# Two-layer hybrid attention and mixture-of-experts kernel: softmax inverse sums spread on VectorE and turned by one transpose; last token tile of the mixing stage done by halves

## What is computed

```python
s = jnp.concatenate([s_loc.reshape(bsz, rows, GRID_W, H, n_loc), s_ctx], axis=-1)
p = jax.nn.softmax(s, axis=-1).astype(v.dtype)
out = (jnp.einsum('brqhkw,brkwhd->brqhd', p_loc, vb)
       + jnp.einsum('brqhk,bkhd->brqhd', p_ctx, v_ctx))
```

```python
x = x + g1 * merge_branches(...)
h2 = modulate(rmsnorm(x, norm2_g[l]), sh2, sc2).reshape(bsz * L, d)
s = jax.nn.sigmoid((h @ router_w).astype(jnp.float32))   # then top-1 group, top-2 experts
```

## Time and profile before

| | us |
|---|---|
| median of 3 runs | 3292.83 (3286.64 to 3298.44) |
| the profiled execution, its own time | 3285.09 |
| its span, first to last instruction | 3283.3 |
| TensorE busy | 3161.9 (96%), 16228 matmul passes |
| VectorE busy | 1649.9 (50%) |
| ScalarE busy | 891.3 (27%) |
| GpSimd busy | 858.3 (26%) |
| mean granted TensorE clock | 0.984 of full |
| attention, first layer | about 380 to 550 |
| attention, second layer | about 2129 to 2282 |
| last tile of mixing, first layer | 1202 to 1222 |
| last tile of mixing, second layer | 2759 to 2779 |

### The profile page before, as it was taken

The page is one execution under the profiler, slowest core; times in us unless marked ns, Lnnn a source line. Parts: engine busy times, 40 slices in busy tenths (PEclk is TensorE's granted clock), DMA queues, the critical chain, the costliest instruction groups (busy, mean ns, idle before and its releaser), DMA issues. The chain is left out here.

```text
span 3283.3 us, 47029 instructions
## 1 busy us (share of the span) xinstructions
PE 3161.9 (96%) x16228; PEld 2440.5 (74%) x16229; DVE 1649.9 (50%) x2422; ACT 891.3 (27%) x1675; POOL 858.3 (26%) x536
## 2 busy tenths in 40 slices
PE   7999999999999999999999999999999989999998
PEld 5887688777777887667666888688778778666665
DVE  4562366666632576433544565166222246887640
ACT  4321265111111332222222332156112132222222
POOL 0140000111011125444444023000111112676664
PEclk9999999999999999999999999999999998999999
DMA  6122243344424246656787522152111134798853
GB/s 263 56 90 106 85 132 97 130 132 135 132 65 153 97 167 227 231 175 210 257 281 249 186 77 103 63 147 85 52 43 51 47 139 181 279 341 285 286 177 83
DMA packets 157387, 500.45 MB, mean 152 GB/s; under 512 B 30498, under 2 KB 81314, under 8 KB 133924
## 3 DMA queue, kind: packets, MB, share of 16 engines
q1 hardware_dynamic: 110880, 394.83, 32.6%
q0 software_dynamic: 17568, 59.82, 8.0%
q10 hardware_dynamic: 28804, 43.98, 4.3%
HBM read 422.51 MB, written 76.39 MB: 152 GB/s over the span
## 5 line engine op out<-in xcount | busy, mean ns | idle before, releaser
L218 PE MATMUL wide<-part,part 128*128 128x512 f32 (+2 forms) x2416 | 974.5, 403 | 28.2 <-DVE part L2632 13.8
L220 PE MATMUL wide<-part,part 128*128 128x512 f32 (+2 forms) x2416 | 929.3, 385 | 0.0
L219 PE MATMUL wide<-part,part 128*128 128x512 f32 (+2 forms) x2384 | 915.2, 384 | 0.0
L218 PEld LDWEIGHTS wide<-part,part 128*128 128x128 f32 x2416 | 458.2, 190 | 139.0 <-issue 47.0
L219 PEld LDWEIGHTS wide<-part,part 128*128 128x128 f32 x2384 | 453.0, 190 | 99.9 <-issue 17.7
L220 PEld LDWEIGHTS wide<-part,part 128*128 128x128 f32 x2416 | 457.6, 189 | 92.1
L1811 POOL TENSOR_TENSOR place<-place,place 128x512 f32 (+3 forms) x80 | 106.2, 1328 | 1080.3 <-DVE place L1775 1080.3
L2630 DVE CAST part<-place 128x2048 fp32r<-128x2048 f32 x128 | 192.4, 1503 | 382.7 <-DMA place<-in_w 376.8
L2492 PE MATMUL bank<-place,place 128*128 x832 | 365.9, 592 | 3.9 <-ACT place L2586 2.7
L2632 DVE TENSOR_TENSOR part<-place,part 128x2048 fp32r<-128x2048 f32 x128 | 349.7, 2732 | 4.4
L2492 PEld LDWEIGHTS bank<-place,place 128*128 128x128 f32 x832 | 154.0, 190 | 178.5 <-issue 178.5
(11 more groups left out here) (272 smaller groups left out, 4067.0 us busy)
## 6 DMA issues: line engine op xcount, KB each, us to landing
place<-in_w SPq DMA_DIRECT2D x118, 1024.0 KB, 13.7
place<-in_w SPq DMA_DIRECT2D x35, 2048.0 KB, 9.6
place<-in_ada_w ACTq DMA_DIRECT2D x72, 512.0 KB, 4.3
place<-in_w_gates SPq DMA_DIRECT2D x32, 640.0 KB, 4.2
place<-in_bias SPq DMA_DIRECT2D x96, 192.0 KB, 3.5
place<-in_ada_w SPq DMA_DIRECT2D x6, 2048.0 KB, 16.9
place<-in_w_rows SPq DMA_DIRECT2D x6, 2048.0 KB, 8.8
place<-in_w_gates SPq DMA_DIRECT2D x16, 768.0 KB, 4.5
```

The costliest lines, as they stand in the source:

```text
L218: pe.matmul(out, left[0], right[0], start=first, stop=False)
L219: pe.matmul(out, left[0], right[1], start=False, stop=False)
L220: return pe.matmul(out, left[1], right[0], start=False, stop=last)
```

## The change

In the attention, VectorE's reciprocal of a tile now writes 128 columns instead of 2: each of the two sums is read 64 times over and its inverse goes into a tile `inv` of its own, three of them in turn. One full transpose of `inv` takes the place of the two products. VectorE waits in addition for the transpose of three tiles before, since the buffer is used again.

In the mixing stage, the last token tile's square sum is taken in two halves, with the table of the root loaded ahead and that of the sigmoid behind; its `norm` passes run over two halves of 512 columns; TensorE may turn the first half when that is ready, and VectorE does these passes behind `choose` but ahead of the passes for the weights and the count, which are now `weigh`.

```diff
+    inv = [place(at + 32 + b * P, P) for b in range(3)]
...
-                ri = st[n % 4][:, 6:8].unsqueeze(2).broadcast_to([P, 2, 64])
-                for h in range(2):
-                    mm = pe.matmul(banks[6][64 * h:64 * h + 64, 2 * P:3 * P], ri[:, h], ident[:], start=True, stop=True)
-                mm.then_inc(s_t[2], 1)
+                pe.transpose(banks[6][:, 2 * P:3 * P], inv[n % 3], ident[:]).then_inc(s_t[2], 1)
...
                 dve.wait_ge(s_pr, 2 * n + 2)
-                dve.reciprocal(x[:, 6:8], x[:, 4:6]).then_inc(s_ri, 1)
+                if n >= 3:
+                    dve.wait_ge(s_t[2], n - 2)
+                dve.reciprocal(inv[n % 3].rearrange("p (h d) -> p h d", d=64),
+                               x[:, 4:6].unsqueeze(2).broadcast_to([P, 2, 64])).then_inc(s_ri, 1)
...
-                sp.wait_ge(s_h2, t + 1)
+                sp.wait_ge(s_h2, t + 1 if t < NQ - 1 else NQ + 1)
...
+                    if t == NQ - 1 and h:
+                        pe.wait_ge(s_h2, NQ + 1)
...
+            def square_half(h):
+
+                t, cs = NQ - 1, slice(h * 512, (h + 1) * 512)
+                act.wait_ge(s_x, order(t, h) + 1)
+                act.activation(junk[t - 1 + h][:, cs], X[t % 3][:, cs], ACT.Square, accum_out=sqh[:, h:h + 1]).then_inc(s_sq, 1)
+                act.wait_ge(s_sq, t + h + 1)
+
+            def norm_first_half():
+                t = NQ - 1
+                act.activation(sqh[:, 2:3], s["eps"][:, 0:1], ACT.Sqrt)
+                square_half(0)
+                act.activation(sq[:, t:t + 1], sqh[:, 0:1], ACT.Identity, bias=s["eps"][:, 0:1], scale=1.0 / D)\
+                    .then_inc(s_half, 1)
+
+            def norm_second_half():
+                t = NQ - 1
+                square_half(1)
+                act.wait_ge(s_half, 1)
+                act.activation(root[:, t:t + 1], sqh[:, 1:2], ACT.Sqrt, bias=sq[:, t:t + 1], scale=1.0 / D)\
+                    .then_inc(s_rt, 1)
+                act.activation(sqh[:, 3:4], s["eps"][:, 0:1], ACT.Sigmoid)
...
-                dve.scalar_tensor_tensor(H2[t % 3], X[t % 3], rstd[:, t:t + 1], mul[:, w], ALU.mult, ALU.mult)\
-                    .then_inc(s_a, 1)
-                dve.wait_ge(s_a, t + 1)
-                dve.tensor_tensor(H2[t % 3], H2[t % 3], add[:, w], ALU.add).then_inc(s_h2, 1)
+                parts = 2 if t == NQ - 1 else 1
+                for h in range(parts):
+                    cs = slice(h * D // parts, (h + 1) * D // parts)
+                    dve.scalar_tensor_tensor(H2[t % 3][:, cs], X[t % 3][:, cs], rstd[:, t:t + 1], mul[:, w, cs],
+                                             ALU.mult, ALU.mult).then_inc(s_a, 1)
+                    dve.wait_ge(s_a, t + h + 1)
+                    dve.tensor_tensor(H2[t % 3][:, cs], H2[t % 3][:, cs], add[:, w, cs], ALU.add).then_inc(s_h2, 1)
...
                 if i % 2 and i >= 3:
                     choose(i // 2 - 1)
+                if i == NQ - 1:
+                    norm(i)
+                if i % 2 and i >= 3:
+                    weigh(i // 2 - 1)
```

More of the change, by code:

```diff
@@ L1865, in mix_and_route @@
     one, wd, fd = cell(2), cell(2, 2), cell(2, 2)
-    sq, root, rstd = cell(NT), cell(NT), cell(NT)
+    sq, root, rstd, sqh = cell(NT), cell(NT), cell(NT), cell(4)
     sc2 = cell(KD, 2)
@@ L1879, in mix_and_route @@
     s_sq, s_rt, s_r, s_a, s_h2 = sem("squares2"), sem("root2"), sem("rstd2"), sem("rows_scaled2"), sem("h2_ready")
+    s_half = sem("half_square")
     s_tn, s_tc, s_lg, s_sg = sem("h2_turned"), sem("h2_turned_copied"), sem("logits"), sem("router_scores")
@@ L2107, in _ @@
                     score(i // 2 - 1)
+                if i == NQ - 1:
+                    norm_first_half()
                 if i - 1 < NQ:
                     copy_turned(i - 1)
-                if i < NQ:
+                if i < NQ - 1:
                     norm(i)
+                elif i == NQ - 1:
+                    norm_second_half()
         @block.vector
@@ L2174, in choose @@
             def choose(p):
-                Sc, to = S[p % 2], OH[p % 2]
+                to = OH[p % 2]
                 for j in range(2):
@@ L2188, in choose, with weigh @@
                 dve.tensor_tensor(M[p % 2].rearrange("p t e -> p (t e)"), to[:, 0], to[:, 1], ALU.add).then_inc(s_m, 1)
+            def weigh(p):
+                Sc, to = S[p % 2], OH[p % 2]
                 do(dve.tensor_tensor(T2, Sc.rearrange("p t e -> p (t e)").unsqueeze(1).broadcast_to([P, 2, 2 * EXP]),
@@ L2241, in _ @@
                     update(i, 0)
-                if i - 1 < NQ:
+                if i - 1 < NQ - 1:
                     norm(i - 1)
```

## The result

| | before | after |
|---|---|---|
| median of 20 runs each, us | 3287.74 (3282.10 to 3298.44) | 3294.16 (3285.31 to 3304.62) |
| the profiled execution, us | 3285.09 | 3300.11 |
| its span | 3283.3 | 3298.3 |

The ratio of the two is 1.0017, 95% interval 1.0009 to 1.0024: the changed kernel is slower by 5.6 us (3.0 to 7.9; the medians themselves are 6.4 apart). The sign is the forecast's, the size is not: +12.9 us was forecast. The interval leaves no change out, but the loss is smaller than the 0.3% (9.9 us) that the prediction took as the least that can be told. The forecast time, 3305.7 us, is too high by another 5.1 us, because it was set on the median of three runs, 3292.83. The profiled execution is one of the longer ones, 6 us over its median, so its span must not be read as the size of the change.

The account below looks back on a forecast made before the run. TensorE was taken to set the steady attention tile (3.99 us), the VectorE-ScalarE ring close behind. First layer +8.1, second +4.8, mixing 0: +12.9 us, set on the median 3292.83, gives 3305.7 us (+0.39%), range 3289 to 3320.

Parts of the forecast that it names:

- The price of the reciprocal: VectorE in attention: the reciprocal over 128 columns takes 0.95 us, longer by 0.785 us in each of the 72 tiles.
- The first rival: Attention: the reciprocal streams like a plain pass (0.32 us); 3288 us, or 3285 with idle products at full clock; chance 0.11.
- the third: Attention: the reciprocal costs more a column than from two to eight, 1.23 us; 3321 us; chance 0.10.
- The ring's local tile: Local attention tile: lengthened by the full 0.785 us, from 3.35 to 4.13 us, above TensorE's 3.88.
- the ring: VectorE and ScalarE in attention: reciprocal, bias pass, exponential of head 0, copy, exponential of head 1, next reciprocal; 3.35 us before.
- The first pairs and the ends of the stages: Attention stages: first pair -0.3 us in the first layer, +0.5 in the second; each end +0.7 for the last reciprocal.
- TensorE's saving: TensorE in a steady attention tile: one transpose for four passes, 0.11 us less, 3.88 instead of 3.99.
- So the saving on TensorE is lost as waiting: Local attention tiles: the ring sets 4.13 us against TensorE's 3.88, 0.14 more than now.
- TensorE waiting about 0.25 us a tile ahead of L1356: Steady attention tiles: expected sign of the forecast, TensorE waiting there for the reciprocal.
- The other steps of a pair: Attention: turning step with 16 transposes 6.53 to 5.89 us, two steps behind it unchanged, two context tiles 5.60 to 5.85.
- Mixing: Mixing stage: rows ready some 1.2 us earlier, but idle products hide the gain; 0 in each layer, at most -1.6 us.
- the second rival: Forecast's attention, but the mixing gain is seen since the clock falls elsewhere; 3302.5 us; chance 0.07.

## Why the prediction was right, and where it was wrong

**The price of the reciprocal: right.** 951 ns against 0.95 us. From eight columns to 128 that is (951 - 203) / 120 = 6.2 ns a column, so the slope of the small passes, 6.7, nearly holds. That 0.95 was hit to the nanosecond is in part luck: the rows' own slope gave 1.00, and the step down from it leaned on durations of two decimals. The first rival (0.32 us) and the third (1.23) are out.
**The ring's local tile, "3.35 + 0.785 = 4.13": the step that failed.** The kind of step was right: a tile is now the ring. The term was mis-sized: the sum took the whole longer duration of the pass as longer ring. The ring grew by 0.65 us to 4.00, since the bias pass starts 0.08 us before the end of the long reciprocal and is 0.06 us shorter behind it. That is 0.13 us a tile. The forecast had put 5 tiles of a middle pair at 4.13 and 9 and 8 of the last ones, 37 in all: 0.13 x 37 = 4.8 us, against a miss of 12.9 - 8.5 = 4.4 in the stages of the attention part. By place: the steady tiles cost +0.01 us and not +0.14, a pair of the first layer +1.53 and not +2.1, its last pair +2.5 and not +3.5, a pair of the second layer +0.2 and not +0.8. The sum was a small difference between two near limits (4.13 and 3.99), so 0.13 us in one of them took all of the steady tiles' part. The range named 0.05 us a tile for this, which was too small. The first pairs and the ends of the stages, the roughest of the estimates, nearly cancel: +0.49 and -0.05 us for the first pairs (-0.3 and +0.5 forecast), and the ends below. For the first pairs that is luck, since they vary by more.

**TensorE's saving: right in size.** 0.11 us and a tile of 3.88 show where the reciprocal is small. "So the saving on TensorE is lost as waiting": right but for 0.7 us, which the stages are longer behind the first pairs when the products are kept. "TensorE waiting about 0.25 us a tile ahead of L1356": wrong place and size. It waits 0.17 us ahead of the scores (L1332) for the bias pass that frees their bank; the turning step comes later in the tile and finds the reciprocal done.

**The other steps of a pair: right.** The step with the 16 transposes takes 5.88 (5.89 forecast), the two behind it 4.82 and 5.21 as before, the two context tiles 5.88 (5.85). The reciprocals of the changed kernel at these places answer to the earlier trace rows: 468.95 and 474.83 around the context tiles, 490.89 and 496.77 around the turning:

```profile
468.95 0.95 DVE L1442 RECIPROCAL place<-place 128x128 f32<-128x128 f32 x1 [0.43 <-ACT place L1505]
...
474.83 0.94 DVE L1442 RECIPROCAL place<-place 128x128 f32<-128x128 f32 x1
...
490.89 0.95 DVE L1442 RECIPROCAL place<-place 128x128 f32<-128x128 f32 x1 [0.43 <-ACT place L1505]
496.77 0.94 DVE L1442 RECIPROCAL place<-place 128x128 f32<-128x128 f32 x1
```

At the ends of the stages it costs 0.78 and 0.45 us (0.7 forecast for each).

**Mixing: right for the reason given, and the second rival seen in part.** The rows are ready 1.0 us earlier (1.2 forecast) and nothing follows from it where the idle products ahead run at half clock. In the changed kernel's own trace these ran at another clock in each layer:

```profile
1223.21 2.03 PE L226 MATMUL wide<-ident 128*128 128x128 f32 x16
1224.69 0.69 DVE L2182 TENSOR_TENSOR place<-place,place 128x512 f32<-128x512 f32 x1
1225.08 1.04 PE L1991 MATMUL bank<-ident,place 128*128 128x128 f32 x8
...
2780.22 2.92 PE L226 MATMUL wide<-ident 128*128 128x128 f32 x16
```

With 2.03 us for the 16 passes instead of 3.76 the transposes of the first layer started early, and the scores were there 10.93 us after the last product pass began, against 13.76 before. Only half of that is the change's. The kernel with the two products kept has the mixing code of before, and in its first layer the idle passes ran at full clock too:

```profile
1218.15 2.03 PE L226 MATMUL wide<-ident 128*128 128x128 f32 x16
1221.38 1.09 PE L1991 MATMUL bank<-ident,place 128*128 128x128 f32 x8 [1.19 <-DVE place L2153]
```

There TensorE waits 1.19 us for the rows, and the transposes start 3.23 us after the idle passes began; in the changed kernel 1225.08 - 1223.21 = 1.87. So with the clock equal the change gives 1.4 us, near the 1.6 that the prediction named for this case, and the other 1.4 are the clock's. In the second layer the scores were 1.1 us earlier than before, with 2.92 us for the passes instead of 3.76; against the first layer of the kernel with the attention part alone (mixing code of before, 2.96 us) the changed kernel's logits end 0.3 us earlier. The mixing stages took 180.02 and 151.09 us against 181.16 and 151.02 before, which is less than they differ with the same code. The clock under the idle products differs between kernels whose mixing stages share their code (3.76 us with the mixing part alone) and between the layers of one trace; what sets it was not looked into. The medians with the mixing part and without it don't differ.

**What stays open.** In the profiled execution of the changed kernel the first pair of the first layer took 3.5 us more, because the weight load of the first weighted products waited for the loads of V:

```profile
396.46 2.00 PEld L1372 LDWEIGHTS bank<-place,place 128*64 128x64 f32 x20 [3.52 <-DMA place<-v_rows]
```

Before it was 1.46 us at this place, and the 20 loads took 1.07 us at full clock, here 2.00 at half. The kernel with the attention part alone has the same attention stage and did not show it (its first layer took 177.65 us, the changed kernel's 180.61). The kernel with two idle products has the attention of before and did: 2.49 us of the same wait, and 1.99 for the loads. So it comes and goes between executions and is not the change's. The stages say +8.5 us, or 8.0 without the first pairs; the timed runs say +7.6 for the attention part and +5.6 for both (intervals 3.6 to 11.5 and 3.0 to 7.9). The first holds the 8.0, the second ends just under it. Whether the mixing part gives back some of it is below what these runs can tell.

## What to carry to other kernels

Before a pass is widened to save another engine some passes, find the ring that it lies in and compare that ring with the period of the engine to be relieved: here 0.62 us of slack stood against 0.785 us of added work, for a saving of 0.11. When two limits come out within some per cent of each other, price the added pass by the distance between the starts of its neighbours and not by its duration, and give the difference an error of its own. Keep a costly operation on the few columns that differ and spread its result by a plain copy, on that engine where the ring has room for it (here 0.2 us) or on one that idles at that point; here the two came out alike. And compare two traces at a place only after the clock there has been seen to be the same.

## What the runs showed of the hardware

- VectorE's reciprocal costs by the column: 153, 163, 203 and 951 ns for 1, 2, 8 and 128 columns, 6.2 ns a column from 8 to 128. The 128 columns were two elements per row, each read 64 times; no run has the reciprocal of 128 different ones. The plain copy of the same 128 columns took 0.23 us on VectorE and 0.29 on GpSimd.
- A pass behind a long one overlapped it more: behind the reciprocal of 0.17 us the bias pass starts 0.02 us before its end and lasts 0.82, behind that of 0.95 us it starts 0.08 before its end and lasts 0.76. A reciprocal behind another one lasted 0.90 us instead of 0.95. No run shows why.
- The same 16 idle passes took 3.76 us (clock 0.50) in one trace and 2.03 (1.00) in another, with the mixing code of before as with the changed one. With four of them instead of 16, the 16 small passes of the logits took 3.59 us instead of 1.96, in both layers.
